# An attention, recurrence and expert block in fp32 parts: query and key-score products in two banks each and a list ahead of the expert choice, index tables transposed ahead of the softmax, and another division of the scaled one-hots

## The chip, the cores and the metric

The kernel runs on one core of a Trainium2 chip. The metric is the device time of one launch in microseconds (us); the number given for a kernel is the median of its runs.

## What is computed

Two transformer-like blocks on 512 tokens of width 1024. The first has differential attention, a gated linear recurrence and, at its end, a layer of retrieved experts; the second has a SwiGLU, a mixer and another SwiGLU. The change lies in the expert layer, which the reference writes so (8 heads, 128 keys, 16 best, 16384 experts):

```python
def peer_ffn(h, w_q, sub_keys, u_tab, v_tab):
    q = (hb @ w_q).reshape(PEER_BLOCK, PEER_HEADS, 2, PEER_HALF)
    sc = jnp.einsum('thcd,hcnd->thcn', q, sub_keys)
    s1, i1 = lax.top_k(sc[:, :, 0], PEER_TOPK)
    s2, i2 = lax.top_k(sc[:, :, 1], PEER_TOPK)
    cand_s = s1[..., :, None] + s2[..., None, :]        # 256 a head
    cand_i = i1[..., :, None] * PEER_N_KEYS + i2[..., None, :]
    top_s, pos = lax.top_k(cand_s, PEER_TOPK)
    idx = jnp.take_along_axis(cand_i, pos, axis=-1)
    g = jax.nn.softmax(top_s, axis=-1)
    act = jax.nn.gelu(jnp.einsum('thkd,td->thk', u_tab[idx], hb))
    return jnp.einsum('thk,thkd->td', g * act, v_tab[idx])
```

## The kernel before

Each fp32 product is made of three TensorE matmuls: weights and activations are held as a high part (rounded to fp32r) and a low part (what the rounding left), and `triple` adds high by high, high by low and low by high in one PSUM bank. Weights come in 128x1024 units in a fixed order (`unit_order`). SyncE loads a unit into one of 5 `raw` buffers, ScalarE copies its high part into `whl`, and VectorE or GpSimd (POOL) makes the low part there. `pool_makes_low` says which of the two. `split` lets ScalarE, VectorE and POOL work up to three units ahead of the unit at their place in the program; ScalarE needs the unit five before it to be done on TensorE.

The expert layer does not gather. TensorE multiplies all 16384 expert rows with all 512 tokens (128 units `pu`, 8 steps of three matmuls each, called u steps below), ScalarE puts each unit through gelu, and it is spilled to DRAM (`ad`). Beside that the choice is made for the 8 heads: `pq` makes the queries of one of a head's two lists (8 triples of 512 columns), `sk` the key scores (4 triples of 128 columns), VectorE finds the 16 best of each list (`best16`: MAX, MAX_INDEX, MATCH_REPLACE, MAX, MAX_INDEX, each waiting for the one before), `cand` and `best` do the same for the 256 sums, and `pick` turns positions into indices (scr tiles I1 and I2). `soft` is the softmax of all heads, `over` transposes I1, I2 and the shares TS on TensorE. Then 128 steps follow, each for 4 tokens: `rows` makes one-hots of I1 (`hot1`, in the `rope` tile), scales them by the high and low part of the share (`share`: 4 tokens by 2 parts), and makes one-hots of I2 (`hot2`, tile `hot`); `g` multiplies them on TensorE (L837: 4 matmuls of 256 columns) and `put` adds the parts into `stage` (L1838), which is stored to DRAM (`gd`) every 16 steps. After that the 128 units `pv` are multiplied with act times weight.

The order of all this is written out once, in `peer_order`; each engine walks through the same list and does its own part of each step, in order. The u steps lie between the others as fill for TensorE. Every engine waits on semaphores that count the results of the others. In `recurrence`, `first_attention` and `merge`, ahead of the experts, nothing changes but who makes the low parts of the first `w_pq` units. ScalarE's `weights("w_pq", n)`, which makes high parts ahead, stands ahead of its copy of query n. `norm("2", ...)` and POOL's `squares("2", ...)` make the second normalisation; the first two query products (`two`) run beside it, with the product of its sum of squares (`sum_of`, L590) in their middle.

## Time and profile before

| | |
|---|---|
| median of 3 runs | 3425.68 us (3425.35 to 3426.66) |
| the profiled execution | 3426.54 us, span 3424.7 us |
| TensorE busy | 3224.3 us (94%) |
| VectorE busy | 2007.3 us (59%) |
| ScalarE busy | 1331.8 us (39%) |
| POOL busy | 650.5 us (19%) |
| matmul groups of L561 to L563 in the chain that ended last | 70% |

Busy time is the union of an engine's instructions. Matmuls overlap in the pipeline, so their spacing says more than their durations. Times in rows count from the start of the span.

### The profile page before, as it was taken

How to read it: one execution, taken by the hardware profiler on the slowest of the kernel's cores; microseconds unless marked ns; L12 is line 12 of the kernel's file. 1: busy time of each engine (PE TensorE's matmuls, PEld its weight loads, DVE VectorE, ACT ScalarE, POOL GpSimd, SP SyncE). 2: the span in 40 equal slices, each digit the busy share in tenths (PEclk: the TensorE clock that was granted, in tenths of full speed). 3: DMA queues.
4: the chain of work that ended last, by engine and by line, in shares of the span. 5: the costliest groups of instructions: out<-in, count | busy, mean ns of one | idle time of the engine just before them, and what ended most of it. 6: DMA issues, size and time to landing. Idle time of an engine off the chain costs nothing.

```text
span 3424.7 us, 37231 instructions
## 1 busy us (share of the span) xinstructions
PE 3224.3 (94%) x14368; PEld 2620.0 (77%) x14368; DVE 2007.3 (59%) x3327; ACT 1331.8 (39%) x2411; POOL 650.5 (19%) x598
## 2 busy tenths in 40 slices
PE   8989999989999899999999999999999987899998
PEld 6767777778887677777788888888888865678887
DVE  5653454548778588887455555554544567544443
ACT  4653445432222377776322222222322233532221
POOL 0000000053443177775000000002000344030000
PEclk9999999999999999999999999999999996789999
DMA  4222111323333356676865555542322320022221
GB/s 138 94 91 92 56 56 56 126 85 129 111 135 110 114 160 183 187 202 177 295 210 197 194 192 191 192 152 86 105 98 92 114 74 13 13 74 99 99 99 62
DMA packets 271200, 424.17 MB, mean 124 GB/s; under 512 B 144816, under 2 KB 148400, under 8 KB 271024
## 3 DMA queue, kind: packets, MB, share of 16 engines
q1 hardware_dynamic: 271024, 421.80, 37.2%
q8 instruction: 114, 1.87, 0.2%
q14 instruction: 62, 0.51, 0.0%
HBM read 348.87 MB, written 72.88 MB: 123 GB/s over the span
## 4 chain that ended last, share of the span: by engine, by line
PE 73%; DVE 13%; ACT 7%; DMA 3%; POOL 3%; issue 1%; SPq 0%; ACTq 0%; POOLq 0%; DVEq 0%
PE pb L561 24%; PE pb L562 23%; PE pb L563 23%; DVE ST L1514 3%; ACT scr L1071 3%; DMA ad<-scr 2%; PE pb L837 1%; ACT share L1324 1%; DVE S L1514 1%; POOL whl L2060 1%; ACT whl L1074 1%; DVE ST L1522 1%; DVE su L1740 1%; DVE su L1743 1%; ACT S L1074 1%
## 5 line engine op out<-in xcount | busy, mean ns | idle before, releaser
L561 PE MATMUL pb<-H,whl 128*128 128x512 f32 x2416 | 972.9, 403 | 32.7 <-ACT scr L1071 14.8
L562 PE MATMUL pb<-H,whl 128*128 128x512 f32 x2416 | 958.5, 397 | 0.0
L563 PE MATMUL pb<-H,whl 128*128 128x512 f32 x2416 | 956.9, 396 | 0.0
L1514 DVE TENSOR_TENSOR whl<-raw,whl 128x1024 fp32r<-128x1024 f32 (+4 forms) x468 | 555.0, 1199 | 347.2 <-ACT whl L1074 346.4
L1074 ACT ACTIVATE whl<-raw 128x1024 fp32r<-128x1024 f32 (+3 forms) x550 | 542.4, 1003 | 506.4 <-PE pb L563 500.9
L561 PE MATMUL pb<-S,whl 128*128 128x512 f32 (+1 forms) x1716 | 671.1, 391 | 25.4 <-DVE whl L1514 11.6
L562 PE MATMUL pb<-S,whl 128*128 128x512 f32 (+1 forms) x1716 | 667.7, 389 | 0.0
L563 PE MATMUL pb<-S,whl 128*128 128x512 f32 (+1 forms) x1716 | 667.3, 389 | 0.0
L561 PEld LDWEIGHTS pb<-H,whl 128*128 128x128 f32 x2416 | 464.3, 192 | 133.5 <-ACT scr L1071 16.4
L563 PEld LDWEIGHTS pb<-H,whl 128*128 128x128 f32 x2416 | 463.8, 192 | 100.6
L562 PEld LDWEIGHTS pb<-H,whl 128*128 128x128 f32 x2416 | 463.8, 192 | 91.9 <-issue 3.2
L561 PEld LDWEIGHTS pb<-S,whl 128*128 128x128 f32 x1716 | 324.5, 189 | 96.1 <-issue 14.7
L562 PEld LDWEIGHTS pb<-S,whl 128*128 128x128 f32 x1716 | 324.7, 189 | 67.0 <-issue 1.0
L563 PEld LDWEIGHTS pb<-S,whl 128*128 128x128 f32 x1716 | 324.4, 189 | 66.7
L2084 POOL TENSOR_TENSOR pad<-X 128x512 f32<-128x512 f32 x32 | 48.1, 1505 | 1643.3 <-DVE X L1514 1614.2
L2075 POOL TENSOR_SCALAR rope<-cst,scr 128x128 f32<-128x128 f32 x384 | 273.9, 729 | 44.8 <-ACT share L1324 43.5
L2060 POOL TENSOR_TENSOR whl<-raw,whl 128x1024 fp32r<-128x1024 f32 x82 | 197.8, 2421 | 374.9 <-ACT whl L1074 374.6
L1514 DVE TENSOR_TENSOR X<-X,pb 128x512 f32<-128x512 f32 x144 | 98.0, 687 | 163.0 <-PE pb L563 160.3
L1514 DVE TENSOR_TENSOR scr<-pb,scr 128x512 f32<-128x512 f32 x96 | 66.1, 691 | 212.4 <-PE pb L563 201.9
L1324 ACT ACTIVATE share<-rope,high 128x128 fp32r<-128x128 f32 x384 | 150.2, 391 | 91.5 <-POOL rope L2075 73.5
L1071 ACT ACTIVATE scr<-pb 128x512 f32<-128x512 f32 x130 | 76.8, 591 | 277.9 <-PE pb L563 257.3
L1838 DVE TENSOR_REDUCE ST<-pb 128x512 f32<-128x1024 f32 x128 | 155.4, 1214 | 0.8 <-PE pb L837 0.8
(193 smaller groups left out, 2990.1 us busy)
## 6 DMA issues: line engine op xcount, KB each, us to landing
raw<-in_pu SPq DMA_DIRECT2D x128, 512.0 KB, 3.6
raw<-in_pv SPq DMA_DIRECT2D x128, 512.0 KB, 4.4
raw<-in_w_in SPq DMA_DIRECT2D x72, 512.0 KB, 3.6
ad<-scr SPq DMA_DIRECT2D x128, 256.0 KB, 3.6
gd<-ST SPq DMA_DIRECT2D x8, 4096.0 KB, 20.7
GA<-gd SPq DMA_DIRECT2D x60, 512.0 KB, 4.6
GA<-ad SPq DMA_DIRECT2D x60, 512.0 KB, 6.3
raw<-in_wg SPq DMA_DIRECT2D x44, 512.0 KB, 3.2
```

The costliest lines, as they stand in the source:

```text
L561: e.matmul(o, lh, h, start=start, stop=False, skip_group_check=True)
L562: e.matmul(o, lh, l, start=False, stop=False, skip_group_check=True)
L563: return e.matmul(o, ll, h, start=False, stop=stop, skip_group_check=True)
L837: last = e.matmul(bank[b + u // 2][:, 256 * (u % 2):256 * (u % 2) + 256], hot2[n % 2][:, 128 * u:128 * u + 128], share[n % 2][:, 256 * u:2 ...
L1071: return e.activation(o, x, func, **kw)
L1074: return e.activation(o, x, ACT.Copy)
L1324: last = e.activation(hot_share(n, u, part), hot1[n % 2][:, 128 * u:128 * u + 128], ACT.Copy, scale=s)
L1514: return e.tensor_tensor(o, x, y, op)
L1838: e.tensor_reduce(stage[n // 16 % 2][:, :, 4 * g:4 * g + 4].rearrange("p i u -> p u i"), pb_t[:, b:b + 1024].rearrange("p (u e i) -> p u i ...
L2060: e.tensor_tensor(wlo(j), raw(j), f(whi(j)), ALU.subtract).then_inc(pool_lo.up(("low", j)), 1)
L2075: last = e.tensor_scalar(hot1[n % 2][:, 128 * u:128 * u + 128], iota, I1[:, 4 * n + u:4 * n + u + 1], None, ALU.is_equal)
L2084: e.tensor_tensor(one_sq if k else sum_sq, x, x, ALU.mult).then_inc(pool.up(), 1)
```

## The change

`pool_makes_low` now names the units `w_pq` from the third on, `pu` 3 to 45, and every second `pu` below 116 (0 and 2 among them); `w_pq` 0, `w_pq` 1 and `pu` 1 go to VectorE. `pq` and `sk` of a list have a bank each for list 0 and list 1, and stand one head ahead of VectorE's search, which is now a step `top` of its own. `over` of I1 and I2 stands ahead of `soft` and waits for the last picks. In `rows` VectorE makes `hot1` in one instruction for three tokens and `hot2`; ScalarE scales five of the eight parts in place of six; POOL, which made the three `hot1` before, makes the other three scaled parts straight from the iota, by a compare and a product in one instruction; VectorE made two such before. ScalarE's `weights("w_pq", n)` stands behind its copy of query n. All else of the computation is the same.

```diff
-    return name == "w_pq" or name == "pu" and (i < 48 or i < 120 and i % 4 == 0)
+    return name == "w_pq" and i > 1 or name == "pu" and (2 < i < 46 or i < 116 and i % 2 == 0)
...
+    out.append(("pq", 0, 0))
+    u(16)
+    out.append(("sk", 0, 0))
+    u(3)
+    out.append(("sk", 0, 1))
+    u(3)
     for h in range(8):
         for c in range(2):
-            if (h, c) != (0, 1):
-                out.append(("pq", h, c))
-            u(16 if h == 0 else 7 if c else 10)
-            out.append(("sk", h, c))
-            u(8 if h == 0 else 5 if c else 3)
-        for step in (("cand", h), ("best", h), ("pick", h, 0), ("pick", h, 1)):
+            if h < 7:
+                out.append(("pq", h + 1, c))
+            u(1)
+            out.append(("top", h, c))
+            u(2)
+            if h < 7:
+                out.append(("sk", h + 1, c))
+        for i, step in enumerate((("cand", h), ("best", h), ("pick", h, 0), ("pick", h, 1))):
             out.append(step)
-            u(6)
-    out.append(("soft",))
-    u(34)
-    for z in range(3):
+            u(10 - i % 2)
+    for z in range(2):
         out.append(("over", z))
         u(6)
+    out.append(("soft",))
+    u(20)
+    out.append(("over", 2))
+    u(10)
...
+        pq_bank, sk_bank = (2, 6), (3, 7)
...
-                            q.wait_ge(dve, ("pq", n - 1))
-                            linear(j, bank[2], Hh, Hl, h2, ("pq", n))
+                            q.wait_ge(dve, ("pq", n - 2))
+                            linear(j, bank[pq_bank[c]], Hh, Hl, h2, ("pq", n))
...
-                        q.wait_ge(dve, ("top", n - 1) if n else ("bra", 7))
+                        q.wait_ge(dve, ("top", n - 2) if n > 1 else ("bra", 7))
+                        if n == 1:
+                            q.wait_ge(act, ("rstd", "2"))
...
-                        q.wait_ge(dve, "soft")
+                        q.wait_ge(dve, ("pick", 7, z) if z < 2 else "soft")
...
+                        q.wait_ge(pool, ("share", n))
...
-                        copy(qh[c], bank[2]).then_inc(act.up(("pq_hi", n)), 1)
+                        copy(qh[c], bank[pq_bank[c]]).then_inc(act.up(("pq_hi", n)), 1)
+                        weights("w_pq", n)
...
-                        q.wait_ge(pool, ("hot1", n))
+                        q.wait_ge(dve, ("hot1", n))
                         q.wait_ge(act, "share_hi")
                         for u in range(3):
-                            for part in range(2):
+                            for part in range(u // 2, 2):
...
+                    elif what == "top":
+                        h, c = step[1:]
+                        n = 2 * h + c
                         q.wait_ge(prod, ("sk", n))
                         for b in range(4):
-                            best16(vals[:, c, b, :], idxu[:, c, b, :], bank[3][:, 128 * b:128 * b + 128], sc2, ("top", n))
+                            best16(vals[:, c, b, :], idxu[:, c, b, :], bank[sk_bank[c]][:, 128 * b:128 * b + 128], sc2, ("top", n))
...
+                            q.wait_ge(act, ("share", n - 2))
+                        tt(hot1[n % 2].rearrange("p (u i) -> p u i", u=3), iota.unsqueeze(1).to_broadcast([128, 3, 128]),
+                           I1[:, 4 * n:4 * n + 3].unsqueeze(2).to_broadcast([128, 3, 128]), ALU.is_equal).then_inc(
+                            dve.up(("hot1", n)), 1)
+                        if n > 1:
                             q.wait_ge(prod, ("g", n - 2))
                         tt(hot2[n % 2].rearrange("p (u i) -> p u i", u=4), iota.unsqueeze(1).to_broadcast([128, 4, 128]),
-                           I2[:, 4 * n:4 * n + 4].unsqueeze(2).to_broadcast([128, 4, 128]), ALU.is_equal)
-                        k = 4 * n + 3
-                        ts(hot_share(n, 3, 0), iota, I1[:, k:k + 1], ALU.is_equal, high_share(k), ALU.mult)
-                        ts(hot_share(n, 3, 1), iota, I1[:, k:k + 1], ALU.is_equal, low_share(k), ALU.mult).then_inc(
+                           I2[:, 4 * n:4 * n + 4].unsqueeze(2).to_broadcast([128, 4, 128]), ALU.is_equal).then_inc(
                             dve.up(("hot2", n)), 1)
...
-                        q.wait_ge(dve, ("over", 1))
+                        q.wait_ge(dve, ("over", 2))
                         if n > 1:
-                            q.wait_ge(act, ("share", n - 2))
-                        for u in range(3):
-                            last = e.tensor_scalar(hot1[n % 2][:, 128 * u:128 * u + 128], iota,
-                                                   I1[:, 4 * n + u:4 * n + u + 1], None, ALU.is_equal)
-                        last.then_inc(pool.up(("hot1", n)), 1)
+                            q.wait_ge(prod, ("g", n - 2))
+                        for u, part in ((2, 0), (3, 0), (3, 1)):
+                            k = 4 * n + u
+                            last = e.tensor_scalar(hot_share(n, u, part), iota, I1[:, k:k + 1],
+                                                   (high_share, low_share)[part](k), ALU.is_equal, ALU.mult)
+                        last.then_inc(pool.up(("share", n)), 1)
```

TensorE's instructions are the same in kind and number. Three places of the new order matter. The first is VectorE at the end of `merge`, where X gets the last products of `w_out`. Before:

```order
L1514 TENSOR_TENSOR whl<-raw,whl 128x1024 [waits weight_high_parts]
L1514 TENSOR_TENSOR X<-X,pb 128x512 [waits x_landed2,pe_products]
L1522 SCALAR_TENSOR_TENSOR S<-X,prm,S 128x512 [waits act_results]
L1514 TENSOR_TENSOR X<-X,pb 128x512 [waits pe_products]
L1522 SCALAR_TENSOR_TENSOR S<-X,prm,S 128x512 [waits act_results]
L1514 TENSOR_TENSOR X<-X,pb 128x512 [waits x_landed3,pe_products]
```

With the change:

```order
L1529 TENSOR_TENSOR whl<-raw,whl 128x1024 [waits weight_high_parts]
L1529 TENSOR_TENSOR X<-X,pb 128x512 [waits x_landed2,pe_products]
L1537 SCALAR_TENSOR_TENSOR S<-X,prm,S 128x512 [waits act_results]
L1529 TENSOR_TENSOR whl<-raw,whl 128x1024 [waits weight_high_parts]
L1529 TENSOR_TENSOR X<-X,pb 128x512 [waits pe_products]
L1537 SCALAR_TENSOR_TENSOR S<-X,prm,S 128x512 [waits act_results]
L1529 TENSOR_TENSOR whl<-raw,whl 128x1024 [waits weight_high_parts]
L1529 TENSOR_TENSOR X<-X,pb 128x512 [waits x_landed3,pe_products]
```

Two low parts (`w_pq` 0 and 1) have come to stand between the additions.

The second is VectorE between two heads, from the end of a pick to the first search of the next list (`S<-pb,S` makes the low part of a query). Before:

```order
L1514 TENSOR_TENSOR ST<-ST,sm 128x256 [waits dve_results] x4
L1801 TENSOR_REDUCE scr<-ST 128x4x16 [waits dve_results]
L1514 TENSOR_TENSOR whl<-raw,whl 128x128 [waits weight_high_parts,dve_results]
L1514 TENSOR_TENSOR S<-pb,S 128x512 [waits act_results]
L1514 TENSOR_TENSOR whl<-raw,whl 128x128 [waits weight_high_parts]
L1739 MAX sm<-pb 128x8 [waits pe_products]
```

With the change:

```order
L1529 TENSOR_TENSOR ST<-ST,sm 128x256 [waits dve_results] x4
L1820 TENSOR_REDUCE scr<-ST 128x4x16 [waits dve_results]
L1529 TENSOR_TENSOR whl<-raw,whl 128x128 [waits weight_high_parts,dve_results]
L1529 TENSOR_TENSOR S<-pb,S 128x512 [waits act_results]
L1754 MAX sm<-pb 128x8 [waits pe_products]
```

The rows are nearly the same, but the query before the search is now that of the next head, and the scores that the search waits for were made a head earlier.

The third is the loop of `rows`, `g` and `put` on VectorE. Before:

```order
L1514 TENSOR_TENSOR hot_60<-cst_61,scr_56 128x512
L1519 TENSOR_SCALAR share_57<-cst_61,scr_56,high_58 128x128
L1519 TENSOR_SCALAR share_57<-cst_61,scr_56,rope_63 128x128
L1838 TENSOR_REDUCE ST_55<-pb 128x4x128
L1514 TENSOR_TENSOR whl_50<-raw_49,whl_50 128x1024
```

With the change:

```order
L1859 TENSOR_REDUCE ST_55<-pb 128x4x128
L1529 TENSOR_TENSOR whl_50<-raw_49,whl_50 128x1024
L1529 TENSOR_TENSOR rope_63<-cst_61,scr_56 128x384
L1529 TENSOR_TENSOR hot_60<-cst_61,scr_56 128x512
```

and POOL in the same loop, a step with the change (before it were three rows L2075 `rope<-cst,scr`):

```order
L2097 TENSOR_SCALAR share_57<-cst_61,scr_56,high_58 128x128 [waits pe_products]
L2097 TENSOR_SCALAR share_57<-cst_61,scr_56,high_58 128x128
L2097 TENSOR_SCALAR share_57<-cst_61,scr_56,rope_63 128x128
L2081 TENSOR_TENSOR whl_50<-raw_49,whl_50 128x1024 [waits weight_high_parts]
```

Two scaled parts have left VectorE and one one-hot of 384 columns has come; POOL's three instructions write `share`, wait for TensorE's `g` two steps before and no longer for ScalarE, and a low part stands in the list every fourth step, where it stood every eighth or ninth.

## Rows read from the trace of the kernel before

**Rows 1.** Windows: us, busy (x count) of PE, PEld, DVE, ACT, POOL, then PEclk
```profile
1191.00:1595.00 404.00, 376.13 (x1831) 314.01 (x1832) 351.04 (x531) 302.06 (x844) 296.43 (x383) 0.98 0.63 182
...
1679.00:2350.00 671.00, 671.00 (x2955) 555.41 (x2954) 373.19 (x370) 191.70 (x188) 0.00 (x0) 1.00 0.55 191
```

**Rows 2.** TensorE's waits in 711:749, 749:1144, 1144:1191, 1191:1595: us, times, longest
```profile
PE pb L561 <- POOL whl L2060: 7.4, 2, 6.8
...
PE pb L561 <- DVE S L1514: 11.6, 7, 4.4
...
PE pb L561 <- ACT scr L1071: 12.1, 1, 12.1
...
PE pb L837 <- ACT share L1324: 27.3, 15, 3.9
```

**Rows 3.** Timeline at the first query products: start us, duration us, engine, operation
```profile
715.12 9.76 POOL L2060 TENSOR_TENSOR whl<-raw,whl 128x1024 fp32r<-128x1024 f32 x4
...
726.84 1.02 PE L590 MATMUL pb<-pad,cst 128*128 128x512 f32 x2
```

**Rows 4.** Timeline of TensorE: a score product, u steps at half clock, a g
```profile
747.39 0.22 PE L561 MATMUL pb<-whl,S 128*128 128x128 f32 x1
...
748.57 0.28 PE L563 MATMUL pb<-whl,S 128*128 128x128 f32 x1
...
1157.38 0.63 PE L561 MATMUL pb<-H,whl 128*128 128x512 f32 x1
...
1157.80 0.63 PE L562 MATMUL pb<-H,whl 128*128 128x512 f32 x1
...
1224.27 0.64 PE L837 MATMUL pb<-share,hot 128*128 128x256 f32 x4
...
1224.74 0.40 PE L561 MATMUL pb<-H,whl 128*128 128x512 f32 x1
```

**Rows 5.** VectorE in head 2, timeline; then its waits in 801:1101
```profile
863.76 0.30 DVE L1739 MAX8 sm<-pb 128x8 f32<-128x128 f32 x1 [2.29 <-PE pb L563]
...
871.20 0.23 DVE L1777 CAST sm<-su 128x128 f32<-128x128 uint32 x1
...
883.36 0.20 DVE L1518 TENSOR_SCALAR su<-su 128x64 uint32<-128x64 uint32 x1
...
890.23 0.20 DVE L1518 TENSOR_SCALAR su<-su 128x64 uint32<-128x64 uint32 x1
...
895.05 2.20 DVE L1514 TENSOR_TENSOR whl<-raw,whl 128x128 fp32r<-128x128 f32 x1
...
DVE sm L1739 <- PE pb L563: 29.8, 10, 4.7
DVE S L1514 <- ACT S L1074: 13.9, 6, 4.5
```

**Rows 6.** Groups by form, 801:1101 (first row), 1200:1590: busy us, mean ns | idle
```profile
L1514 DVE TENSOR_TENSOR whl<-raw,whl 128x128 fp32r<-128x128 f32 x12 | 11.1, 924 | 0.5 <-ACT whl L1074 0.3
...
L1514 DVE TENSOR_TENSOR whl<-raw,whl 128x1024 fp32r<-128x1024 f32 x41 | 49.9, 1216 | 44.8 <-ACT whl L1074 44.8
...
L1324 ACT ACTIVATE share<-rope,high 128x128 fp32r<-128x128 f32 x351 | 137.4, 391 | 87.1 <-POOL rope L2075 72.8 <-PE pb L837 13.9
...
L2075 POOL TENSOR_SCALAR rope<-cst,scr 128x128 f32<-128x128 f32 x349 | 251.3, 736 | 36.8 <-ACT share L1324 35.7
L2060 POOL TENSOR_TENSOR whl<-raw,whl 128x1024 fp32r<-128x1024 f32 x14 | 33.8, 2414 | 68.8 <-ACT whl L1074 68.8
```

**Rows 7.** Timeline in the loop of one-hots, [idle before <-releaser]
```profile
1212.13 2.47 POOL L2060 TENSOR_TENSOR whl<-raw,whl 128x1024 fp32r<-128x1024 f32 x1 [5.72 <-ACT whl L1074]
...
1212.27 2.42 DVE L1519 TENSOR_SCALAR share<-cst,scr,high 128x128 fp32r<-128x128 f32 x1
...
1478.88 0.60 ACT L1071 ACTIVATE scr<-pb 128x512 f32<-128x512 f32 x1 [4.97 <-DMA ad<-scr]
```

**Rows 8.** POOL's one-input form of two operations, groups by form, whole span
```profile
L2104 POOL TENSOR_SCALAR scr<-pad,prm 128x512 f32<-128x512 f32 x30 | 29.7, 992 | 0.0
```

More of the change, by code:

```diff
@@ L1760, in experts @@
                                 q.wait_ge(prod, ("pq", c))
[L1761 removed]
+                                tt(first_q[c], bank[pq_bank[c]], scr[8], ALU.mult).then_inc(dve.up(("pq_raw", c)), 1)
                             for c in range(2):
@@ L1800, in experts @@
                             then(tt(eq[:, b], eq[:, b], idxf[:, c, b, :].unsqueeze(1).to_broadcast([128, 16, 16]), ALU.mult))
-                        then(e.tensor_reduce((I1v, I2v)[c][:, :, h, :], eq, AX_X, ALU.add))
+                        then(e.tensor_reduce((I1v, I2v)[c][:, :, h, :], eq, AX_X, ALU.add), ("pick", h, c))
                     elif what == "soft":
```

12 lines of the change are left out of this document (6 added, 6 removed).

## The prediction

> **What bounds the kernel now.** I read the page first, then windows by stage, then TensorE's waits in each, then the timeline of every engine around those waits. TensorE is the bound nearly everywhere: in the 671 us behind the expert choice it is busy all the time at the full clock of 2.4 GHz, and its 2955 matmuls stand 0.227 us apart [rows 1]. A u step (three) is thus 0.68 us, a query product or unit 5.45, a head's score product about 1.35, and the four matmuls of a `g` 0.47 [rows 4]. The change leaves TensorE's work alone, so it can only give back what TensorE waits, and what the clock and pipeline lose behind a wait. Behind a long wait the granted clock is at its lower level, 1.2 GHz, for a while: u matmuls then stand 0.43 us apart in place of 0.227 [rows 4], 0.20 lost on each. Each resumed stream also loses about 0.2 us in refilling. The waits lie in four places [rows 2]: 7.4 us ahead of the first query products, 11.6 in the heads, 12.1 at the softmax, 27.3 in the loop of one-hots (29.4 with a first wait of 2.1 for VectorE).
>
> **The change part by part.** My sum goes by counted events in the timeline.
>
> *(a) First query products.* POOL makes four low parts in a row from 715.12 on, when its squares are done, and TensorE, which ended `w_out` at 711.2, waits 6.8 and 0.7 us for the first two [rows 2, 3]. With the change VectorE makes both while `w_out` still runs: the added rows of the order stand ahead of X 5 and X 6, and their high parts are there by then. VectorE has over 2 us free in each of those 5.4 us, and this is the cover; without it each costs 1.2 [rows 6]. The two query products then run from 711.2 to 722.4. The sum of squares in their middle (L590) comes at 716.7, not 726.84 [rows 3], still later than POOL's last square at 715.1. All that hangs on it (ScalarE's root, VectorE's normalisation, the first u steps) comes 10.1 us earlier: 7.4 of waiting, 2.6 of half clock (13 matmuls), a refill. What is new is `pu` 1, whose low part VectorE makes only behind its normalisation: 0 to 1.2 us of waiting [rows 6]; I take 0.8. Gain 9.3.
>
> *(b) Heads.* VectorE's head was about 50 us long, of which 43.7/6 = 7.3 were waits for TensorE's scores and ScalarE's query [rows 5]: a query product, then fill, then scores, each in turn. TensorE's own head was 49 u steps, 10.9 of query and 2.7 of scores: 47.0, so it waited about 1.6 us for the low part of the query. Now the scores lie ready a head earlier and the fill is 44 u steps: TensorE's head is 30.0 + 10.9 + 2.7 = 43.6. VectorE's is two searches of 7.44, sums and best of 12.16, two picks of 4.82 [rows 5], two query parts of 0.69 and two key parts of 0.28: 38.5 clean. To that come stalls behind POOL. A pick took 6.87 in place of 4.82, and a key part 2.20; the twelve key parts average 0.924 against 0.28 clean [rows 5, 6]. Over six heads VectorE's own time was 50 - 7.3 = 42.7, so the stalls are 4.2 a head. VectorE needs 42.7 where TensorE needs 43.6, and the margin in between (the query is ready 0.5 us before it is needed) makes some 1.5 in all. Most heads pass without a wait; a head with 6 us of stalls costs 0.5. I take 2 us in all.
>
> A new wait takes the place of the old ones in heads 0, 2, 4 and 6. There a new `pu` unit begins at the third u step between `pq(h+1,0)` and `sk(h+1,0)`, so the next query unit is the third behind the first. ScalarE now makes its high part only after its copy of the first query, and POOL's low part of 2.4 follows [rows 6]: 0.7 + 1.05 + 2.45 = 4.2 us after the first query product. TensorE needs it after three u steps and the scores, 3.4. That is 0.8 and a refill, 1.0, four times: 4.0. Before, 11.6 of waits came with 4.7 of half clock on u matmuls (23), 2.2 on scores and 7 refills: 19.9 in all. After: 6.0. Gain 14.
>
> *(c) End of the choice.* Head 7 has no query products ahead of it, so its fill is 30 us, and VectorE's share of it is 36.6 and stalls. From the end of the last list-0 query product TensorE needs 38.1 + 30.0 = 68.1 us to `over 0`; times here count from the end of that product. VectorE starts its second search of head 6 at 10.2, ends head 6 at 42.7, and with 27.0 to `best` of head 7, one `pu` low part of 1.2, the first pick of 4.8 and 2 of stalls it ends that pick at about 77.7. TensorE waits 9.5 there, then for half a microsecond at `over 1`, and runs at half clock for 12 matmuls again. The old wait was 12.1 with 12 such matmuls [rows 2]. So the transposes before the softmax do not remove the stall, they replace it. Gain 2.
>
> *(d) Loop of one-hots.* The old waits come every 28 us: POOL's low part of 2.4 (every fourth unit) delays its three `hot1`, ScalarE waits 72.8 us for these, and TensorE for ScalarE [rows 2, 6, 7]. Now POOL's part goes straight to TensorE, may start when `g` two steps before is done, and is needed 5.9 us later. POOL per step: three instructions at 0.736 and a low part of 2.41 every 3.94 steps, 2.21 + 0.61 = 2.82. TensorE per step: 4.06 u steps and a `g`, 2.77 + 0.50 = 3.27. POOL is at 86% (before 73% [rows 1]), and even a step with a low part, 2.4 + 2.2 behind the high part, ends about a microsecond ahead of need. ScalarE falls from six to five parts of 0.39; VectorE, busy 87% [rows 1], trades two small one-input instructions for one of 384 columns and loses a third of its low parts. What stays is the spill: ScalarE waited 4.97 us for `ad` beside the stores of `gd`, and TensorE lost 3.9 by it [rows 2, 7]. Three units now pass in 19.3 us in place of about 20.4, so this wait grows by about 1.1 each time, but ScalarE's slack is larger. I take 5 us of waits and clock from it, and 1.5 at the first `g`, where POOL has a low part and three products to do within TensorE's ten u steps. Before: 29.4 + 5.6 half clock (28 matmuls) + 3.2 refills = 38. After 6.5 to 7. Gain 31.
>
> **A price that the trace lacks.** POOL's new instruction compares, multiplies and writes fp32r. The nearest row below is the compare alone at 0.736, and above is mult and add over 512 columns at 0.992 [rows 6, 8], four times as wide. I take 0.75, since the second operation cannot cost much where 512 columns fit into 0.99. At t us POOL's step is 3t + 0.61; it becomes the bound from t = 0.89 on, and at 0.99 the loop is 127 x 0.31 = 39 us longer.
>
> **Sum.** 9.3 + 14 + 2 + 31 = 56. The profiled execution took 3426.5 (span 3424.7 and 1.8 around it), so 3370.5; the median of the runs is 0.9 lower. I predict 3370.
>
> **A rule weighed.** The row first: a one-input instruction of VectorE took 2.42 us when it met a POOL low part that had begun 0.14 us before it, and ended with it [rows 7]. The Trainium skill, SBUF — State Buffer, Who interferes with whom, calls this an exclusive lock of a shared port pair, which a VectorE instruction with two SBUF inputs also needs against a POOL instruction that reads. By that rule `hot1` on VectorE and twice as many low parts on POOL speak against the change. From rows: 15 more low parts of POOL in the loop, each stalling VectorE by up to 2.4 us, are 36 us over 128 steps, 0.28 a step; VectorE, 2.88 of 3.31 now, would come to 3.16, still under TensorE's 3.27. It would decide only with a further 0.11 a step. As to the price above, the same skill's GPSIMD Engine Reference, Elementwise — side-by-side cycle accounting, says that bodies of up to two operations are bound by the port, which would make the second operation free; no run here shows it yet.
>
> **Rivals.**
> - *POOL becomes the bound in part*: its instruction takes 0.95, so the step is 3.46 and the loop gives 24 us less: 3394. For it: a second scalar pointer, an fp32r output. Against it: 0.992 for four times the columns. Chance 0.12.
> - *VectorE is late in every head*: the stalls come to 6.5 a head, TensorE waits 2 us in each head with half clock behind it, and (b) gives nothing: 3384. For it: TensorE's margin is 1.5 us. Chance 0.1.
> - *More comes back*: spills and the first `g` cost nothing, `over 0` waits 5: 3355. Chance 0.1.
> - *Slower*: POOL's instruction takes over 1.05 us. At 1.1 its step is 3.91, the loop is 127 x 0.64 = 81 us longer than in the main case, and the time is 3451. It decides from 1.04 on, where the loop eats the 56 us of all gains. Chance 0.05.
> - *No effect*: POOL at 1.02 to 1.05, or losses of several kinds that meet. The change does what it says on each engine, so a pure nothing is unlikely. Chance 0.03.
>
> **How the numbers follow.** The main case has 0.6 and its own range is 3358 to 3382. With the late heads and half of the partly bound POOL at the upper side and the larger gain at the lower, 3352 to 3396 holds 0.8. Within 0.2% (7 us) is about what a measurement of this kernel cannot tell from no change. Faster 0.92, same 0.03, slower 0.05.
>
> **What would show it.** L590 near 716.7 and no wait for POOL before it. Heads 43.6 to 44.6 us apart, VectorE's waits for scores in them near nothing, four waits of TensorE for a POOL low part near 0.8 us. One wait of 8 to 12 us at the first transpose. POOL's new instruction near 0.75 us, POOL busy near 86% of the loop, at most three or four TensorE waits in it. Wrong if POOL's instruction is over 0.89, or if TensorE waits for VectorE's query in most heads.

## The result and the profile after

The changed kernel takes 3558.05 us (median of 4 runs, 3555.61 to 3559.14) beside 3425.51 for the kernel before (4 runs, 3422.07 to 3426.66). The ratio is 1.0388, with a 95% interval of 1.037 to 1.0406: 132.5 us slower, where 3370 was forecast. The profiled execution has a span of 3556.3 us.

Page of the kernel after, parts 1, 2 and 4: busy time, the granted clock in 40 slices, and the chain that ended last.

```profile
PE 3255.1 (92%) x14368; PEld 2636.3 (74%) x14368; DVE 2037.3 (57%) x3187; ACT 1300.5 (37%) x2283; POOL 811.1 (23%) x610
...
PEclk9999998988898999999999999999999996789999
...
PE 69%; POOL 13%; DVE 10%; ACT 5%; issue 1%; DMA 1%; SPq 0%; DVEq 0%; ACTq 0%; POOLq 0%
PE pb L572 23%; PE pb L573 22%; PE pb L574 22%; POOL share L2097 11%; ACT scr L1085 2%; POOL whl L2081 2%; DVE S L1529 1%; ACT S L1088 1%; DVE ST L1529 1%; DVE ST L1537 1%; DVE su L1755 1%; DVE su L1758 1%; DVE ST L1756 1%; DMA ad<-scr 1%; DVE sm L1757 1%
```

TensorE has the same 14368 matmuls. Two things are new: POOL's line of scaled parts (L2097) is 11% of the chain, and the granted clock is lower in most slices of the heads (the ninth to the thirteenth), where the kernel before has 9 in all. The windows of the kernel after say where (columns as in [rows 1]):

```profile
690.00:730.00 40.00, 38.49 (x162) 29.40 (x160) 24.98 (x30) 13.61 (x19) 18.40 (x11) 1.00 0.09 30
...
760.00:1160.00 400.00, 307.56 (x1258) 253.91 (x1257) 252.19 (x736) 71.84 (x103) 106.69 (x45) 0.86 0.26 85
...
1200.00:1740.00 540.00, 484.19 (x2298) 391.48 (x2297) 424.28 (x535) 313.49 (x792) 490.95 (x419) 1.00 0.57 164
```

In the heads TensorE is busy 77% of the time at a granted clock of 0.86, and VectorE 63%: neither is full. In the loop POOL is busy 91% of a window that is a little longer than the loop. TensorE's waits in 690:760, 760:1160, 1160:1250 and 1250:1760 answer to [rows 2]:

```profile
PE pb L572 <- DVE su L1758: 6.8, 1, 6.8
...
PE pb L572 <- DVE su L1758: 91.3, 12, 9.9
...
PE pb L841 <- DVE scr L1820: 3.8, 1, 3.8
PE pb L841 <- DVE scr L1834: 2.5, 1, 2.5
...
PE pb L851 <- POOL share L2097: 47.4, 60, 1.3
```

A further one of 6.8 us for L1758 lies in the third window. So 104.9 us in 14 waits go to the last instruction of a search, which stood in no wait of before. The timeline of VectorE and TensorE around the third of these, at the first score product of head 2, shows what it is:

```profile
813.33 0.69 DVE L1529 TENSOR_TENSOR S<-pb,S 128x512 fp32r<-128x512 f32 x1 [7.06 <-ACT S L1088]
814.14 0.29 DVE L1754 MAX8 sm<-pb 128x8 f32<-128x128 f32 x1
...
821.23 0.28 DVE L1758 FIND_INDEX8 su<-sm,ST 128x8 uint32<-128x128 f32 x1
835.58 0.69 DVE L1529 TENSOR_TENSOR S<-pb,S 128x512 fp32r<-128x512 f32 x1 [14.06 <-ACT S L1088]
...
814.24 0.39 PE L574 MATMUL pb<-H,whl 128*128 128x512 f32 x1
821.66 0.44 PE L572 MATMUL pb<-whl,S 128*128 128x128 f32 x1 [7.03 <-DVE su L1758]
821.90 0.42 PE L573 MATMUL pb<-whl,S 128*128 128x128 f32 x1
...
825.22 0.63 PE L574 MATMUL pb<-H,whl 128*128 128x512 f32 x1
825.64 0.63 PE L572 MATMUL pb<-H,whl 128*128 128x512 f32 x1
```

`sk` of the next head overwrites the bank that the search of the same list in this head reads. That search begins at 814.14, right behind the low part of the query that TensorE has just made, and takes 7.4 us. TensorE has three u steps (2.0 us) for it, so it stands until 821.66, and its u matmuls then stand 0.43 us apart, at the lower level of the clock. The next query product stands behind this score product in TensorE's list, so VectorE waits in turn: 14.06 us at 835.58, 130.5 us for ScalarE's copies of the query in the heads. Each engine stands while the other works. Starts of score products of list 0 lie 66.1 and 63.9 us apart in turn (821.66, 887.75, 951.60), where 43.6 was forecast.

The other new wait, in the loop, as a timeline of VectorE, POOL and TensorE and as groups by form (1266:1742):

```profile
1401.41 1.23 DVE L1529 TENSOR_TENSOR whl<-raw,whl 128x1024 fp32r<-128x1024 f32 x1 [1.39 <-ACT whl L1088]
1402.55 0.55 DVE L1529 TENSOR_TENSOR rope<-cst,scr 128x384 f32<-128x384 f32 x1
1403.02 0.68 DVE L1529 TENSOR_TENSOR hot<-cst,scr 128x512 fp32r<-128x512 f32 x1
...
1410.85 2.41 DVE L1529 TENSOR_TENSOR rope<-cst,scr 128x384 f32<-128x384 f32 x1
...
1400.23 0.79 POOL L2097 TENSOR_SCALAR share<-cst,scr,rope 128x128 fp32r<-128x128 f32 x1
1401.00 0.79 POOL L2097 TENSOR_SCALAR share<-cst,scr,high 128x128 fp32r<-128x128 f32 x1
1401.78 2.43 POOL L2097 TENSOR_SCALAR share<-cst,scr,high 128x128 fp32r<-128x128 f32 x1
1404.19 0.79 POOL L2097 TENSOR_SCALAR share<-cst,scr,rope 128x128 fp32r<-128x128 f32 x1
...
1410.44 2.41 POOL L2081 TENSOR_TENSOR whl<-raw,whl 128x1024 fp32r<-128x1024 f32 x1
...
1405.13 0.70 PE L851 MATMUL pb<-share,hot 128*128 128x256 f32 x4 [0.52 <-POOL share L2097]
...
L2097 POOL TENSOR_SCALAR share<-cst,scr,high 128x128 fp32r<-128x128 f32 x254 | 294.9, 1168 | 0.0
L2097 POOL TENSOR_SCALAR share<-cst,scr,sm 128x128 fp32r<-128x128 f32 x64 | 59.0, 922 | 0.0
L2097 POOL TENSOR_SCALAR share<-cst,scr,rope 128x128 fp32r<-128x128 f32 x64 | 54.3, 849 | 0.0
```

POOL's scaled part takes 0.79 us where VectorE has no two-input instruction running (1400.23), and also where one starts beside it later (1401.00: VectorE's low part starts at 1401.41). It takes 2.43 where one is running when it starts and two more follow (1401.78): it ends 0.5 us behind the last of the three. So it goes through the loop: the 180 parts that started while a two-input instruction of VectorE ran took 1.38 us on average; 132 beside which one started later took 0.81 (all but four of them 0.79 or 0.80), the rest 0.79. The mean is 1.07, with no idle time before any: POOL bounds the loop. POOL's low part at 1410.44 in its turn holds VectorE's one-hot until it ends (2.41 for 0.55).

Two numbers hold the whole loss: the start of the first `g`, and the time from it to the last `g`. The list of before has 51 more u steps (34.7 us) ahead of the first `g` and 48 fewer (32.6) in the loop, so the forecast was 1191.3 - 34.7 - 25.3 = 1131.3 for the first, and 421.3 + 32.6 - 31 = 422.9 for the second.

| | first `g` starts | first to last `g` | whole, us |
|---|---|---|---|
| before | 1191.3 | 421.3 | 3425.5 |
| forecast | 1131.3 | 422.9 | 3370 |
| after | 1266.9 | 475.4 | 3558.1 |

That is 135.6 us in the heads and 52.5 in the loop, 188 in all, which is the distance from 3370 to 3558.

### The profile page after: what moved, and what is told of

Read it like the earlier page. It is cut to its first block, busy times and chain, and to the rows that moved or that the text cites. A ratio compares the mean times of both kernels' runs of the same rounds, so it can differ in the third digit from the quotient of the medians.

```text
span 3556.3 us, 37117 instructions
## 1 busy us (share of the span) xinstructions
PE 3255.1 (92%) x14368; PEld 2636.3 (74%) x14368; DVE 2037.3 (57%) x3187; ACT 1300.5 (37%) x2283; POOL 811.1 (23%) x610
## 4 chain that ended last, share of the span: by engine, by line
PE 69%; POOL 13%; DVE 10%; ACT 5%; issue 1%; DMA 1%; SPq 0%; DVEq 0%; ACTq 0%; POOLq 0%
PE pb L572 23%; PE pb L573 22%; PE pb L574 22%; POOL share L2097 11%; ACT scr L1085 2%; POOL whl L2081 2%; DVE S L1529 1%; ACT S L1088 1%; DVE ST L1529 1%; DVE ST L1537 1%; DVE su L1755 1%; DVE su L1758 1%; DVE ST L1756 1%; DMA ad<-scr 1%; DVE sm L1757 1%
## 5 line engine op out<-in xcount | busy, mean ns | idle before, releaser
L1088 ACT ACTIVATE whl<-raw 128x1024 fp32r<-128x1024 f32 (+4 forms) x550 | 543.5, 1002 | 591.5 <-PE pb L574 591.2
L1529 DVE TENSOR_TENSOR whl<-raw,whl 128x1024 fp32r<-128x1024 f32 (+4 forms) x456 | 536.4, 1190 | 337.3 <-ACT whl L1088 336.7
L572 PE MATMUL pb<-S,whl 128*128 128x512 f32 (+1 forms) x1716 | 670.7, 391 | 18.0 <-DVE whl L1529 11.7
L572 PEld LDWEIGHTS pb<-H,whl 128*128 128x128 f32 x2416 | 467.2, 193 | 121.1 <-DVE whl L1529 13.6
L2081 POOL TENSOR_TENSOR whl<-raw,whl 128x1024 fp32r<-128x1024 f32 x94 | 225.5, 2412 | 396.8 <-ACT whl L1088 396.6
L2097 POOL TENSOR_SCALAR share<-cst,scr,high 128x128 fp32r<-128x128 f32 x256 | 296.5, 1166 | 0.0
L1529 DVE TENSOR_TENSOR scr<-pb,scr 128x512 f32<-128x512 f32 x96 | 66.1, 691 | 212.3 <-PE pb L574 201.9
L1529 DVE TENSOR_TENSOR S<-pb,S 128x512 fp32r<-128x512 f32 (+3 forms) x81 | 47.9, 591 | 235.8 <-ACT S L1088 235.8
L1339 ACT ACTIVATE share<-rope,high 128x128 fp32r<-128x128 f32 x256 | 101.1, 395 | 162.6 <-DVE rope L1529 125.0
```

Of the source, the lines that this page charges most:

```text
L572: e.matmul(o, lh, h, start=start, stop=False, skip_group_check=True)
L1088: return e.activation(o, x, ACT.Copy)
L1339: last = e.activation(hot_share(n, u, part), hot1[n % 2][:, 128 * u:128 * u + 128], ACT.Copy, scale=s)
L1529: return e.tensor_tensor(o, x, y, op)
L2081: e.tensor_tensor(wlo(j), raw(j), f(whi(j)), ALU.subtract).then_inc(pool_lo.up(("low", j)), 1)
L2097: last = e.tensor_scalar(hot_share(n, u, part), iota, I1[:, k:k + 1], (high_share, low_share)[part](k), ALU.is_equal, ALU.mult)
```

## Experiments

The theory after the trace has two parts. **S**: the score product waits for the search of the same list one head back. **P**: POOL's three scaled parts, each lengthened by VectorE's two-input instructions, are longer than a step. The rivals: for S, that VectorE's work in the heads is too long anyway and a wait goes elsewhere; for P, that the second operation or its pointer is what costs, or POOL's low parts. Runs without an interval are single; the kernel before beside them took 3423.7 to 3425.7 us (medians). In diffs, + and - stand against the changed kernel where nothing else is said.

**e1, four banks for scores.** Each list's bank comes round two heads later.

```diff
-        pq_bank, sk_bank = (2, 6), (3, 7)
+        pq_bank, sk_bank = (2, 6), (3, 7, 4, 5)
...
-                        q.wait_ge(dve, ("top", n - 2) if n > 1 else ("bra", 7))
+                        q.wait_ge(dve, ("top", n - 4) if n > 3 else ("bra", 7))
```

> The changed kernel with the key scores in four banks (3, 7, 4, 5) in place of two; order and all else as changed. Theory S: a score product of the next head waits for VectorE's search of the same list of this head, since it overwrites its bank, and this search has only just begun. The 14 waits of 6.8 to 9.9 us (104.8 in all) and the half clock behind them (24 us on u matmuls, 4 on scores) then go, and the wait at the first transpose grows from 3.8 to about 9.5: 3558 - 125 = 3433, 3422 to 3445. Rival L: VectorE is simply late, by its stalls behind POOL, and PE waits for it whatever the bank; then over 60 us of waits at the scores stay and the time is over 3490.

3456.05 us, 102 less than the changed kernel; first `g` at 1165.2, loop 475.6. TensorE's waits in 760:1240:

```profile
PE pb L572 <- DVE S L1529: 19.9, 6, 4.0
PE pb L841 <- DVE scr L1820: 15.6, 1, 15.6
...
PE pb L572 <- POOL whl L2081: 2.3, 3, 0.8
```

The bank alone made the 104.9 us, and Rival L is out; but 102 us came back where 125 were expected, and 3456 lies outside the 3422 to 3445. What is left are waits for VectorE's part of the query, a new 19.9 us: two waits, of 4.0 and 2.6, in each of heads 2, 4 and 6. The first of them in head 4, on VectorE and TensorE:

```profile
897.99 0.69 DVE L1529 TENSOR_TENSOR S<-pb,S 128x512 fp32r<-128x512 f32 x1
...
898.83 0.45 PE L572 MATMUL pb<-whl,S 128*128 128x128 f32 x1 [4.05 <-DVE S L1529]
```

ScalarE had made the high part at 892.77 to 893.37, but VectorE was still in the pick of the head before, which stands ahead of the query's low part in its list. The score products of list 0 lie 52.2 and 46.2 us apart in turn, 49.2 on average, where 43.6 was forecast: without the bank's wait, the place of the score product still costs. The waits for POOL's low part of 0.8 that the prediction gave are here, with the size that it gave.

**e2, score products late.** Two banks, but `sk` of the next head stands behind `best` and the first `pick` of this one.

```diff
             u(2)
-            if h < 7:
-                out.append(("sk", h + 1, c))
...
             out.append(step)
             u(10 - i % 2)
+            if h < 7 and i in (1, 2):
+                out.append(("sk", h + 1, i - 1))
```

> The changed kernel, two score banks as changed, but the score products of the next head stand behind best and behind the first pick of this head, in place of three u steps behind their query; fill steps as changed. Theory S: the search that a score product waits for is over by then, so the 14 waits (104.8 us) and their half clock go; and since 30 u steps lie between a query and its scores, VectorE's lateness of up to 15 us is hidden too, which in the kernel with four banks still cost 19.9 us. Expected 3456 - 20 - 3 = 3430, 3418 to 3440, the wait at the first transpose 10 to 18. Rival L (VectorE's own time is over TensorE's 43.6 a head): the lateness adds up from head to head and comes out at the first transpose; the time is then 3450 or more.

3433.62 us, first `g` at 1142.9, loop 475.7. The order of the list undoes part S without a further bank: 124 us back, as expected, since the lateness of VectorE that e1 still shows is hidden too. What stays in 760:1140, besides 12.2 at the first transpose:

```profile
PE pb L572 <- DVE whl L1529: 11.7, 3, 3.9
```

The second score product needs the low part of its keys, which VectorE makes only at this step of its list, behind the pick. In both e1 and e2 the loop is as long as in the changed kernel to 0.3 us: S and P are separate.

**e3, POOL compares only.** The product with the share is left out of POOL's three parts.

```diff
-                                                   (high_share, low_share)[part](k), ALU.is_equal, ALU.mult)
+                                                   None, ALU.is_equal)
```

> The changed kernel with POOL's three instructions of a step as a compare alone (the product with the share is left out, so the output is not the reference's). Theory P: the instruction with compare and product takes 1.07 us with its stalls, three of them and a low part make POOL's step 3.8 us and POOL the bound of the loop, 3.74 us a step against TensorE's 3.27. With the compare alone at about 0.74 the loop falls from 475 to about 423 us and the time to 3505. Rival K: what holds the loop is the stall of POOL against VectorE's new one-hot and twice as many low parts; then the instruction hardly gets shorter with its stalls, the loop stays over 455 us, the time over 3538.

3518.73 us, loop 435.4: between the two theories, 12 us above the 423 of the first.

**e13, POOL multiplies by a constant.**

```diff
-                                                   (high_share, low_share)[part](k), ALU.is_equal, ALU.mult)
+                                                   1.0, ALU.is_equal, ALU.mult)
```

> The changed kernel, where POOL's three instructions multiply by the constant 1.0 in place of the share (the share is left out of these parts). It asks what makes POOL's instruction long. If the second operation costs: near 1.07 us on average as in the changed kernel, and 3558. If the second pointer costs: near 0.85 as with the compare alone, and 3519.

3533.81 us, loop 450.8. The forms of POOL in the loop, of e3 and then of e13:

```profile
L2097 POOL TENSOR_SCALAR share<-cst,scr 128x128 fp32r<-128x128 f32 x379 | 315.5, 849 | 8.1 <-PE pb L851 8.0
```

```profile
L2097 POOL TENSOR_SCALAR share<-cst,scr 128x128 fp32r<-128x128 f32 x380 | 373.5, 1000 | 0.7 <-PE pb L851 0.7
```

Neither expectation of e13 was right alone: the mean goes 0.85, 1.00, 1.07 from the compare to the product with a constant to the product with a pointer. The compare of before took 0.736 [rows 6]. What of this is POOL's own work is read from the parts beside which VectorE ran no two-input instruction, one each of the kernel before, e3 and e13 (the changed kernel's is at 1400.23 above):

```profile
1221.60 0.60 POOL L2075 TENSOR_SCALAR rope<-cst,scr 128x128 f32<-128x128 f32 x1
...
1403.82 0.60 POOL L2097 TENSOR_SCALAR share<-cst,scr 128x128 fp32r<-128x128 f32 x1
...
1407.82 0.71 POOL L2097 TENSOR_SCALAR share<-cst,scr 128x128 fp32r<-128x128 f32 x1
```

The medians of all such parts (230, 160, 63 and 69 of them) are 0.60, 0.60, 0.71 and 0.79. So the fp32r output costs nothing, the second operation 0.11, its pointer 0.08. The rest of each mean is standing behind VectorE: 0.14 a part before, 0.25 in e3, 0.29 in e13, 0.28 in the changed kernel.

**e4, two parts on POOL**, six on ScalarE.

```diff
-                            for part in range(u // 2, 2):
+                            for part in range(2):
...
-                        for u, part in ((2, 0), (3, 0), (3, 1)):
+                        for u, part in ((3, 0), (3, 1)):
```

> The changed kernel with two scaled parts on POOL in place of three, and six on ScalarE. Theory P: POOL's step is 2 x 1.07 + 0.61 = 2.75 us, under TensorE's 3.27; ScalarE's is 6 x 0.29 + 0.8, under it too. The loop falls to about 423 us, the time to 3505. Rival K (stalls at the shared data and low parts, not the instructions' own length): POOL's waits stay in over half of the steps, over 3530.

3515.17 us, loop 437.2, waits for POOL 14.1 in place of 47.4. One part moved to ScalarE, which had room, gives 38 of the 52.5 us. The other 14 stay: POOL is no longer full, and yet TensorE waits for it 17 times.

**e5, fewer low parts of POOL in the loop**, every fourth unit in place of every second.

```diff
-    return name == "w_pq" and i > 1 or name == "pu" and (2 < i < 46 or i < 116 and i % 2 == 0)
+    return name == "w_pq" and i > 1 or name == "pu" and (2 < i < 46 or i < 116 and i % 4 == 0 or i in (2, 46, 50, 54))
```

> The changed kernel with every fourth unit's low part on POOL in the loop in place of every second (VectorE makes the others), the choice as changed. Theory P: POOL's step is 3.2 + 0.3 = 3.5 us, still over TensorE's 3.27, so a part of the waits stays: the loop is 445 us or so, the time 3528. Rival K: the low parts are what POOL has no room for; the waits go wholly, the time is 3505.

3543.19 us, loop 463.0, waits for POOL 36.1. The gain of 15 us is half of what P expects, and K's 3505 is out.

**e15, none of them**, three parts on POOL (`i < 54 and i % 2 == 0` in the line above).

> The changed kernel, with POOL's three scaled parts a step and none of its low parts in the loop. Theory A (POOL's low parts are what makes the loop late): POOL's step is then 3 times 1.07 or 3.2 us against TensorE's 3.27, its waits go from 47 to under 10 us, the loop from 475 to 430 us, and the whole is 3513. Theory B (its scaled parts alone bind it, since they take longer the more often VectorE reads beside them): the loop stays over 450 us, and the whole over 3530.

3525.29 us, loop 449.7, on the edge between the two theories. The forms of POOL in this loop (1261:1710):

```profile
L2097 POOL TENSOR_SCALAR share<-cst,scr,high 128x128 fp32r<-128x128 f32 x252 | 304.2, 1214 | 4.7 <-PE pb L851 4.6
L2097 POOL TENSOR_SCALAR share<-cst,scr,sm 128x128 fp32r<-128x128 f32 x64 | 77.6, 1213 | 0.0
L2097 POOL TENSOR_SCALAR share<-cst,scr,rope 128x128 fp32r<-128x128 f32 x62 | 66.3, 1070 | 0.0
```

The low parts are gone and POOL is still nearly full: its parts have grown from 1.07 to 1.19 on average, with 64 low parts of VectorE, two-input instructions too, beside them where there were 34. 3 x 1.19 = 3.57 against a measured step of 3.541. So the price of POOL's part is no constant; it rises with the two-input instructions that VectorE runs.

**e7, score products late and two parts on POOL** (e2 and e4 together).

> Late scores as in the kernel before it, and two scaled parts on POOL in place of three, six on ScalarE. If the two causes S and P are independent, the gain of two parts (3558 - 3515 = 43) comes on top of that of the late scores: 3430 - 43 = 3387. If they share anything (clock, lead of TensorE), it is over 3400.

3400.24 us, first `g` at 1144.7, loop 437.9, and the kernel is under the one before. The loops add up: two parts make the loop 37.8 us shorter than e2's, where they made it 38.2 shorter alone. The whole does not: 33.4 us less than e2, where 43 were expected. In e4 the first `g` also came 6.3 us earlier, which is not explained; here it comes 1.8 later than in e2.

**e9, one part on POOL**, one on VectorE, six on ScalarE, with late scores, and **e10, the loop's division of before** (POOL makes `hot1`, VectorE two parts), with late scores and the low parts of e5.

> Late scores; one scaled part on POOL, one on VectorE, six on ScalarE. With two parts POOL's instruction took 1.14 us on average with its stalls and the loop 3.44 us a step against 3.27 of work. Theory P: with one part POOL's step is 1.1 + 0.6 and the waits for it go; the loop is 3.3 a step, 18 us less than with two parts: 3370. Rival K: the stalls between POOL and VectorE move to VectorE, which gets one more instruction (2.9 of 3.27 us); the loop stays at 3.4 or more, over 3380.

> Late scores, with the division of the loop of one-hots as in the kernel before the change (POOL makes the first one-hots, ScalarE waits for them, a quarter of the low parts on POOL). Theory P: the loop falls from 3.74 to 3.27 + 0.25 us a step, since the stalls of the old loop (29 us of waits and 9 of clock and refill over 127 steps) come back: 3430 - 30 = 3400. If the new division were better but for the length of POOL's instruction, the kernel with one part beats it by 20 us or more.

3408.05 us with a loop of 445.2, and 3401.69 with 440.9. Neither beats two parts on POOL, and between e7 and e10 lie 1.5 us, which single runs do not tell apart: with two parts on POOL the new division of the loop is worth nothing that could be measured over the old one. With one part, where 3370 was expected, POOL still makes TensorE wait 15.9 us in 18 waits.

**e11, e7 with the low parts of e5**, and **e14, with none of POOL's low parts in the loop** (and with the edit of e12).

> The changed kernel with key products behind the search (as in the run with key products late), two scaled parts on POOL, and POOL's low parts in the loop cut to every fourth unit. Theory (POOL's low parts in the loop delay its scaled parts): POOL waits of TensorE fall from 14.8 us to about 8, and the whole is 3394. Rival (VectorE is hit instead, by its own added low parts): waits for VectorE and ScalarE take their place, 3400 or more.

> As the run with key lows on POOL, late keys and two scaled parts, but VectorE makes every low part in the loop of one-hots; POOL makes none there. Theory (every low part of POOL in the loop costs TensorE 1 to 2 us, by standing ahead of POOL's scaled parts and by holding VectorE's one-hots for as long): the waits for POOL and for the one-hots go, the loop of 127 steps goes from 429.9 to 419 us, and the whole is 3386. Rival (VectorE is then too full, 10 to 12 more low parts of 1.2 us on it): VectorE is late, and the loop stays at 430 us or more.

Both theories fell, and in both the time of the rival came: loops of 453.5 and 462.5 us where e7 has 437.9 (whole: 3412.75; and 3403.64, 0.9938 of before, 0.9921 to 0.9954). In e11 the waits for POOL did not fall to 8 us but rose from 14.8 to 21.5, beside 6.3 for VectorE and 6.0 for ScalarE. The timeline of e11 shows what one low part of POOL does there, on VectorE, POOL and TensorE:

```profile
1324.49 2.43 DVE L1529 TENSOR_TENSOR rope<-cst,scr 128x384 f32<-128x384 f32 x1
1326.85 0.68 DVE L1529 TENSOR_TENSOR hot<-cst,scr 128x512 fp32r<-128x512 f32 x1
...
1324.11 2.40 POOL L2081 TENSOR_TENSOR whl<-raw,whl 128x1024 fp32r<-128x1024 f32 x1 [3.63 <-ACT whl L1088]
1326.49 1.62 POOL L2097 TENSOR_SCALAR share<-cst,scr,high 128x128 fp32r<-128x128 f32 x1
1328.10 0.79 POOL L2097 TENSOR_SCALAR share<-cst,scr,rope 128x128 fp32r<-128x128 f32 x1
...
1329.03 0.71 PE L851 MATMUL pb<-share,hot 128*128 128x256 f32 x4 [1.56 <-POOL share L2097]
```

POOL idles 3.63 us, then the low part stands ahead of its two scaled parts, holds VectorE's one-hot, and the delayed `hot` then lengthens the scaled part: 1.56 us on TensorE, though POOL is far from full. Why half as many low parts of POOL cost more than in e7 is not shown by this row; it stays open. With none of them (e14) the waits for POOL go, and other ones come, over the loop (1126:1588):

```profile
PE pb L851 <- DVE rope L1529: 29.3, 46, 1.7
```

VectorE, with every low part of 1.2 us in its list, is late itself. The even division of the changed kernel is the best of the three beside two scaled parts.

**e12, key lows on POOL**, with e11.

```diff
-    return name == "w_pq" and i > 1 or name == "pu" ...
+    return name == "w_pq" and i > 1 or name == "sk" and i > 1 or name == "pu" ...
```

> As the run with late keys, two parts and fewer low parts of POOL, and POOL makes the low parts of the key units too, so that TensorE does not wait for VectorE's place in the list. Theory A (the three waits of 3.9 us are TensorE's own loss): they go with the half clock behind them, 15 us, and the whole is 3381. Theory B (VectorE is what sets the end of the choice, and TensorE only waits elsewhere): the waits go, but the wait at the first transpose grows from 12 to 23 us, and the whole is within 4 us of the run without this edit.

3396.85 us (0.9915 of before, 0.9899 to 0.9932), 15.9 less than e11. The first `g` comes at 1125.3 in place of 1143.3, and the wait at the first transpose stays at 12.5: theory A, and B is out.

**e16, e7 with key lows on POOL**, the loop's low parts as in the changed kernel.

> The changed kernel with late keys, two scaled parts on POOL, key lows on POOL, and the loop's low parts divided as in the changed kernel, every second one on POOL. Its two halves have been seen apart: the loop of the run with two parts (437.9 us from the first to the last product of one-hots) and the heads of the run with key lows on POOL (18 us shorter). If they add up, the whole is 3382. Rival (the loop's waits depend on where it begins against the weight units, so they do not carry over): 3390 or more.

3382.99 us, as expected, and 0.9881 of before (0.9865 to 0.9898): 175 us under the changed kernel and 40.6 under the one before, the lowest time measured. First `g` at 1126.2, loop 440.0. In 760:1080 TensorE waits for nothing. Behind that, in 1080:1250 and 1250:1760:

```profile
PE pb L841 <- DVE scr L1820: 12.5, 1, 12.5
PE pb L851 <- POOL share L2097: 3.6, 3, 3.0
PE pb L851 <- ACT share L1339: 2.5, 1, 2.5
...
PE pb L851 <- POOL share L2097: 11.8, 14, 1.9
```

**e17, more fill in head 7**: 16 u steps more there, 16 fewer in the loop.

```diff
-            u(10 - i % 2)
+            u(10 - i % 2 + (4 if h == 7 else 0))
```

> The same, with 16 more u steps between the steps of head 7 and so 16 fewer in the loop. Theory (head 7 lacks fill, and TensorE's wait of 12.5 us for the last pick is work that was moved to the wrong place): the wait falls to about 2 us, the loop takes 10 us less, and the whole is 3370. Rival (VectorE's work in the loop takes over as the bound once the loop has less fill a step): the loop gets no shorter, waits for VectorE and POOL grow by 10 us, and the whole is as without the edit.

3384.49 us (0.9885, 0.9869 to 0.9902): the rival, within error of e16. The 12.5 us became 6.5, now a wait for one of VectorE's low parts; the loop is only 4.5 us shorter for 10.9 us less work.

**e8, the kernel before with its first two query lows on VectorE**, part (a) alone (+ and - against before).

```diff
-    return name == "w_pq" or name == "pu" and (i < 48 or i < 120 and i % 4 == 0)
+    return name == "w_pq" and i > 1 or name == "pu" and (i < 48 or i < 120 and i % 4 == 0)
```

> The kernel before with one edit: VectorE makes the low parts of the first two query units in place of POOL. Theory (part a of the prediction stands by itself): the waits of 6.8 and 0.7 us for POOL go, the sum of squares comes 10 to 12 us earlier, and the whole is 3414, 10 to 12 us under the kernel before. Rival: the gain is given back at the next wait (VectorE's choice of experts is then later than TensorE's fill, and TensorE waits longer in head 0 and at the softmax), and the whole gains under 3 us.

3412.9 us, 0.9964 (0.9952 to 0.9977), 11.6 less. The first `g` comes 13.6 us earlier, the loop is 421.4 as before. The gain is kept.

## Why the prediction was wrong

**(a) First query products: right in place, a little small.** The sum of squares runs at 715.07 in place of 726.84 [rows 3], no wait for POOL is left, and the wait for `pu` 1 is 0.2 and not 0.8. Forecast 9.3; the edit alone is worth 11.6 (e8).

**(b) Heads: the step that failed.** It said "Now the scores lie ready a head earlier and the fill is 44 u steps: TensorE's head is 30.0 + 10.9 + 2.7 = 43.6". It priced the product and not the bank that it writes: `sk(h+1,c)` waits for `top(h,c)`, which in the new list stands two u steps ahead of it. All numbers for this wait were there: ScalarE's copy of 0.7, the query's low part of 0.69, the key's of 0.28 and the search of 7.44 [rows 5] end 9.1 us behind the query product, three u steps take 2.0, and the difference is 7.1; the third wait is 7.03, all 14 are 6.8 to 9.9. Fourteen of 7.1 are 100 us, with half clock behind each; no rival had it. The bank is worth 101.7 of the 135.6 us by which the first `g` is late (e1).

Of the other 33.9, the waits of e1 for the query's low part are 19.9. So a second reading failed as well, the one that left 2 us for VectorE's lateness because "the query is ready 0.5 us before it is needed": in heads 2, 4 and 6 of e1 it comes 4 us late. In part that is the rival *VectorE is late in every head*, which had 2 us in each. Another 6 us are at the first transpose, 15.6 for 9.5; the rest, with the lower clock behind these waits in it, was not divided. Heads of 43.6 us do exist, but in another list: in e16, with late score products and key lows on POOL, the score products of list 0 start at 815.04, 858.64, 902.24, 43.60 us apart. So the price of TensorE's own work in a head was right, and the claim that this order leaves it free was not. Of the four waits of 0.8 for POOL, e1 shows three, e16 none, since `sk` stands elsewhere.

**(c) End of the choice: right in kind.** The changed kernel waits 3.8 and 2.5 us there, since TensorE comes late. Where the bank's wait is gone and the score products come late, the wait is 12.2 to 12.5 us (e2, e7, e16), forecast 9.5. That the stall is replaced and not removed holds. More fill in head 7 halves it and gains nothing in the whole (e17).

**(d) Loop: the term that was mis-sized.** "POOL per step: three instructions at 0.736 and a low part of 2.41 every 3.94 steps, 2.21 + 0.61 = 2.82" should read 3 x 1.07 + 0.61 = 3.8; measured are 3.743 a step. Of the 0.33 between 0.736 and 1.07, 0.11 are the second operation, 0.08 its pointer, and 0.14 more standing behind VectorE's two-input instructions (e3, e13 and the undisturbed parts beside them). Even 0.79 a part would have made a step of 2.98, under TensorE's 3.27: it is the 0.28 of standing in each part that makes POOL the bound. The prediction's 0.736 held 0.14 of it already, from a loop in which VectorE ran another mix beside it, and it took that over as a constant. The mechanism of the rival *Slower* (over 1.05), which had a chance of 0.05, is what came. By its formula 1.07 makes the loop 127 x 0.55 = 70 us longer than 127 x 3.27; measured are 475.4 - 415.3 = 60.

The condition given, bound from 0.89 on, is not the whole of it. In e3 the part takes 0.85 and in e4 POOL has two, and TensorE still waits 11.7 and 14.1 us for POOL, with loops of 435.4 and 437.2 where 422.9 was forecast. So "even a step with a low part, 2.4 + 2.2 behind the high part, ends about a microsecond ahead of need" was wrong too: the row of e11 shows a low part ahead of two scaled parts and 1.56 us of waiting. The "about 20.4" us for three units before is too small as well, since 24 u steps at 3.69 a step of 3.317 us take 21.6; all waits for ScalarE, those for the spill among them, came to 2.2 us in the changed loop and to 4.1 in e4, where 5 were forecast for the spill with its clock.

**The rule weighed.** The row again: POOL's low part at 1410.44 holds VectorE's one-hot of 0.55 for 2.41. And in the other direction, POOL's part of 0.79 takes 1.62 when VectorE's one-hots of two inputs run (e11, 1326.49). The Trainium skill, SBUF — State Buffer, Who interferes with whom, states both: a VectorE instruction with two SBUF inputs and a POOL instruction that reads contend for one shared port pair, and who comes first decides who stands. The trace agrees for POOL's parts, which kept 0.79 us when VectorE came second, and for the one-hots behind a POOL low part. It differs for one order: 97 of VectorE's one-hots of 384 columns in the loop started while a scaled part of POOL ran, and none took over 0.56 us. I had priced only the direction that stalls VectorE, which had room. On the price of POOL's instruction, the undisturbed parts have 0.60 for one operation, 0.71 for two with a constant and 0.79 for two with a pointer. The Trainium skill, GPSIMD Engine Reference, Elementwise — side-by-side cycle accounting, calls bodies of up to two operations port-bound, which would make these equal; here they were not. Whether the difference grows with the columns or is paid once an instruction no run tells, since all these parts have 128.

What stays open: all that makes up the 14 us of the loop that e3 and e4 leave. A list in which POOL's low parts stand behind its scaled parts was not tried. The runs of more than one edit rest on their neighbours for the share of each edit.

## What to carry to other kernels

When a producer is moved ahead, look at what it overwrites as well as at what it needs: list the readers of that bank in the order of the new program, and price each as start plus duration. When two engines stand in each other's list, a wait of one becomes a wait of the other (104.9 us on TensorE and 130.5 on VectorE here), and the lower clock comes behind it. For an engine whose instructions grow beside a neighbour's, read two prices from the trace, undisturbed and standing, and take the second from a stretch where the neighbour runs what it will run. Before it is given more work, work out the point at which it becomes the bound: here one instruction of eight, moved to an engine with room, was worth 38 us.

## What was not expected of the hardware

- POOL's compare-and-multiply of 128x128 took 0.79 us beside a VectorE that reduces from PSUM or is idle, and up to 2.73 when one of its two-input instructions was running at the start; one that started later cost nothing in 128 of 132 cases. The mean went from 1.07 to 1.19 when POOL's own low parts were given to VectorE (e15).
- Undisturbed, a second operation with a constant cost POOL 0.11 us, a pointer in its place 0.08 more, and an fp32r output nothing.
- Behind a wait of 7.03 us the score matmuls stood 0.21 apart and the nine u matmuls that followed 0.43 (821.66 to 828.20), and over the heads 96 u matmuls stand that far apart; the granted clock of the heads was 0.86, and is 0.98 in e16 over 760:1126.
